# The output projection of a hybrid decoder layer as seven block products, with one sum of weight blocks made on chip

## What is computed

```python
g_nsa, g_sgu = jnp.split(jax.nn.sigmoid(merge_gl), 2, axis=-1)
merged = g_nsa * (o_nsa @ w_branch_nsa[l]) + g_sgu * (o_sgu @ w_branch_sgu[l])
mix = merged @ w_out[l]                                     # 512 x 1024 by 1024 x 1024
h = layer_norm(DEEPNORM_ALPHA * h + mix, ln1_g[l], ln1_b[l])
ffn = (jax.nn.silu(h @ w_ffn_gate[l]) * (h @ w_ffn_up[l])) @ w_ffn_down[l]
h = layer_norm(DEEPNORM_ALPHA * h + ffn, ln2_g[l], ln2_b[l])
```

## Time and profile before

| | |
|---|---|
| median of 3 runs | 712.57 us (712.55 to 713.74) |
| the profiled execution | 713.21 us, span 711.5 us |
| TensorE busy | 700.4 us (98%) |
| VectorE busy | 567.5 us (80%) |
| ScalarE busy | 352.0 us (49%) |
| GpSimd busy | 151.2 us (21%) |
| moved by DMA | 73.84 MB, mean 104 GB/s |
| mean granted TensorE clock | 0.996 |

### The profile page before, as it was taken

The page is one execution under the profiler, slowest core; times in us unless marked ns, Lnnn a source line. Parts: engine busy times, 40 slices in busy tenths (PEclk is TensorE's granted clock), DMA queues, the critical chain, the costliest instruction groups (busy, mean ns, idle before and its releaser), DMA issues.

```text
span 711.5 us, 11496 instructions
## 1 busy us (share of the span) xinstructions
PE 700.4 (98%) x4232; PEld 622.9 (88%) x4232; DVE 567.5 (80%) x918; ACT 352.0 (49%) x552; POOL 151.2 (21%) x167
## 2 busy tenths in 40 slices
PE   8999999999999999999999999999999999999995
PEld 7888988878888988888899899999999998888884
DVE  6885499787788785675889598999898886977877
ACT  6462777457777778222534244444544344145600
POOL 2942970422132210000000222222222210000001
PEclk9999999999999999999999999999999999999998
DMA  9612343111101205536532133233223328400102
GB/s 314 229 45 67 112 119 119 60 59 60 41 20 60 59 1 161 195 119 236 148 90 67 52 119 110 67 118 118 80 96 118 118 78 306 185 23 0 60 31 88
DMA packets 55716, 73.84 MB, mean 104 GB/s; under 512 B 4096, under 2 KB 40704, under 8 KB 55552
## 3 DMA queue, kind: packets, MB, share of 16 engines
q1 hardware_dynamic: 55392, 72.19, 30.6%
q0 software_dynamic: 144, 1.05, 0.7%
q10 hardware_dynamic: 144, 0.13, 0.1%
HBM read 70.21 MB, written 2.10 MB: 102 GB/s over the span
## 4 chain that ended last, share of the span: by engine, by line
PE 96%; DVE 2%; DMA 0%; ACT 0%; issue 0%; DVEq 0%; SPq 0%; ACTq 0%
PE ps L1981 65%; PE ps L2430 10%; PE ps L2064 5%; PE ps L2448 5%; PE ps L1993 4%; PE ps L1989 3%; PE ps L1990 3%; PE ps L2003 1%; PE ps L2421 0%; DMA stage<-in_w_in 0%; DVE ptl L1252 0%; PE ps L2164 0%; PE ps L2165 0%; DVE wl L1252 0%; DVE prob L1533 0%
## 5 line engine op out<-in xcount | busy, mean ns | idle before, releaser
L1981 PE MATMUL ps<-xh,wh 128*128 128x256 f32 (+1 forms) x416 | 135.0, 325 | 0.0
L1981 PE MATMUL ps<-xh,wl 128*128 128x256 f32 (+1 forms) x416 | 131.7, 317 | 0.0
L1981 PE MATMUL ps<-xl,wh 128*128 128x256 f32 (+1 forms) x416 | 131.6, 316 | 0.0
L1981 PE MATMUL ps<-ath,wh 128*128 128x256 f32 (+1 forms) x280 | 86.1, 307 | 0.0
L1981 PE MATMUL ps<-ath,wl 128*128 128x256 f32 (+1 forms) x280 | 86.0, 307 | 0.0
L1981 PE MATMUL ps<-atl,wh 128*128 128x256 f32 (+1 forms) x280 | 86.0, 307 | 0.0
L1981 PEld LDWEIGHTS ps<-xh,wl 128*128 128x128 f32 x416 | 79.3, 191 | 5.4
L1981 PEld LDWEIGHTS ps<-xh,wh 128*128 128x128 f32 x416 | 79.5, 191 | 3.1
L1981 PEld LDWEIGHTS ps<-xl,wh 128*128 128x128 f32 x416 | 79.5, 191 | 3.1
L1252 DVE TENSOR_TENSOR wl<-stage,wh 128x512 fp32r<-128x512 f32 (+2 forms) x73 | 64.6, 897 | 4.9 <-ACT wh L796 2.8
L1242 DVE TENSOR_TENSOR wl<-stage,wh 128x2048 fp32r<-128x2048 f32 (+1 forms) x19 | 43.1, 2267 | 27.8 <-ACT wh L793 19.6
(11 more groups left out here) (374 smaller groups left out, 1741.4 us busy)
## 6 DMA issues: line engine op xcount, KB each, us to landing
stage<-in_w_ffn_gate SPq DMA_DIRECT2D x22, 512.0 KB, 4.5
stage<-in_w_ffn_up SPq DMA_DIRECT2D x22, 512.0 KB, 4.5
stage<-in_w_in SPq DMA_DIRECT2D x20, 512.0 KB, 4.1
stage<-in_w_ffn_down SPq DMA_DIRECT2D x14, 512.0 KB, 4.2
quad_raw<-in_w_in SPq DMA_DIRECT2D x8, 512.0 KB, 9.4
stage<-in_w_out SPq DMA_DIRECT2D x8, 512.0 KB, 4.6
quad_raw<-in_w_ffn_down SPq DMA_DIRECT2D x4, 1024.0 KB, 10.1
arena<-in_x_t SPq DMA_DIRECT2D x8, 256.0 KB, 5.5
```

What stands on the lines that cost most here:

```text
L1981: return pe.matmul(out, (sh, sh, sl)[i], (mh, ml, mh)[i], start=start and i == 0, stop=stop and i == 2)
```

## The change

With merged tokens in two halves and its channels in two halves (blocks S), and `w_out` in four blocks B11, B12, B21, B22 (first index: channels), the product is made from seven block products of 24 matmuls instead of eight. In the order of TensorE, product 1 is S11 B11, product 2 is S12 B21, product 3 is s1 (B11 + B12), product 4 s2 times the sum B22 + B12 + B11, product 5 s4 B22, product 6 s3 (B22 + B12), product 7 S22 times B21 + that sum. `s1` to `s4` are sums or differences of merged blocks, made by VectorE. Results are added into `y` by twelve steps on VectorE (`take`), one of them from a copy of product 1 that ScalarE makes (`first_product`), because product 4 adds onto it in the same banks.

The sums of weight blocks are made by accumulating DMAs of GpSimd (`more`, `more_rows`; each waits for the one before), from `w_out` or from a block on chip. B22 + B12 is copied to `t_3` by SP, the sum of three is made in place on chip. Where a low part is made by DMA, as `second_l` is already, ScalarE writes the negated rounded block first (`negated`): so for products 4 and 7 and for `first_l`. That is eight accumulating DMAs instead of one.

Tiles 2 and 3 are both transposed in the last of the first four FFN tiles, tile 3 in its middle. The `up` tiles of the first FFN unit wait for the last sums out of banks 2 and 3 (`in_out` 14). The loops over `c` of ScalarE and VectorE are written out. SP's and ScalarE's queues are re-ordered as shown.

```diff
@@ SP
             load(U_BRANCH + 2, 0, nsa_rows(512))
-            load(U_BRANCH + 3, 1, rows4(sgu_d, 1, 0, 512, 512))
+            sp.wait_ge(st_done, 4)
+            out_rows(t_sums, 1, 1, 0)
             sp.wait_ge(o_end, PAIRS)
             sp.dma_start(y[:, :, :], x_d).then_inc(x2_arrived, 16)
-            with sp.Fori(0, 2) as c:
-                for kh in range(2):
-                    load(2 * c + U_OUT + kh, kh, rows4(wout_d, kh, kh, 512 * c, 512))
+            load(U_BRANCH + 3, 1, rows4(sgu_d, 1, 0, 512, 512))
+            sp.wait_ge(w_lo, U_BRANCH + 3)
+            out_rows(stage[0][:, :], 0, 0, 2)
+            sp.wait_ge(more_in, 16)
+            for i in range(2):
+                part = slice(1024 * i, 1024 * i + 1024)
+                sp.dma_start(t_3[:, part], t_sums[:, part]).then_inc(raw_arrived[1], 16)
+            sp.wait_ge(mg_ok, 4)
+            out_rows(b_21, 1, 0, 3)
+            load(U_FFN + 1, 1, rows8(up_d, 1, 0))
+            sp.wait_ge(part_lo, 12)
+            load(U_FFN, 0, rows8(gate_d, 0, 0))
+
+            sp.wait_ge(s_sum, 8)
             sp.wait_ge(mg_lo, KD)
...
@@ GpSimd
+            def more(n, dst, src):
+                if n > 1:
+                    pool.wait_ge(more_in, 16 * (n - 1))
+                pool.dma_start(dst, src, accum_op=ALU.add).then_inc(more_in, 16)
...
+            pool.wait_ge(part_lo, 9)
+            more_rows(1, t_sums, 0, 1)
+            pool.wait_ge(raw_arrived[1], 64)
+            more_rows(2, t_sums, 0, 0)
+            pool.wait_ge(part_lo, 10)
+            pool.dma_start(stage[0][:, :].rearrange("p (k n) -> p k n", k=4), wout_d[:, 0:4, 512:1024],
+                           accum_op=ALU.add).then_inc(second_in, 16)
+            pool.wait_ge(part_lo, 11)
+            more(3, b_21, t_sums)
             pool.wait_ge(second_neg, 1)
+            more(4, M_SLOT[0][1], t_sums)
+            pool.wait_ge(second_neg, 2)
+            more(5, M_SLOT[0][1], b_21)
+
+            pool.wait_ge(second_neg, 3)
+            pool.dma_start(first_l[:, :], stage[0][:, :], accum_op=ALU.add).then_inc(second_in, 16)
...
@@ ScalarE
+            late_split(U_BRANCH + 2, 0)
+            out_t_hi(2, t_sums, arrived_in=(0, 64))
+            for f in range(4):
+                merged_hi(f)
+            late_split(U_BRANCH + 3, 1)
+            act.wait_ge(w_used, U_BRANCH + 3)
+            out_t_hi(0, stage[0][:, :], arrived_in=(2, 64))
+            out_t_hi(3, b_21, arrived_in=(3, 64))
+            for f in range(4, 7):
+                merged_hi(f)
+            act.wait_ge(second_in, 16)
+            act.wait_ge(w_used, U_BRANCH + 4)
+            act.copy(M_SLOT[1][0], stage[0][:, :]).then_inc(part_hi, 1)
+            merged_hi(7)
+            act.wait_ge(more_in, 32)
+            act.wait_ge(in_used, 8)
+            negated(M_SLOT[0][1], t_sums)
+            out_s_hi("s1", 6)
+            out_t_hi(0, t_sums, 2)
+            out_s_hi("s2", 7)
+            act.wait_ge(in_used, 9)
+            act.copy(first_product, ps[:, 0:2, :]).then_inc(bank_out, 1)
+            out_s_hi("s4", 8)
+            act.wait_ge(in_used, 10)
+            out_s_hi("s3", 5)
+            out_t_hi(1, t_3, arrived_in=(1, 64))
+            act.wait_ge(more_in, 48)
+            act.wait_ge(in_used, 11)
+            negated(M_SLOT[0][1], b_21)
+            out_t_hi(0, b_21, 3)
+            act.wait_ge(w_arrived[0], arrived(U_FFN)[1])
+            act.wait_ge(part_lo, 13)
+            negated(first_l[:, :], stage[0][:, :])
...
             root(0)
+            split_to(first_h[:, :], U_FFN, 0, U_FFN)
             act.wait_ge(w_arrived[1], arrived(U_FFN + 1)[1])
-            act.mul(second_l[:, :], stage[1][:, :], -1.0).then_inc(second_neg, 1)
-            hi(second_h[:, :], stage[1][:, :]).then_inc(w_hi, 1)
+            negated(second_l[:, :], stage[1][:, :])
             root(1)
             ht_hi_of(0)
+            act.wait_ge(more_in, 80)
+            hi(second_h[:, :], stage[1][:, :]).then_inc(w_hi, 1)
             ht_hi_of(1)
             root(2)
-            split_to(wh[:, 0, :], U_FFN + 2, 0, U_OUT + 3)
+            act.wait_ge(in_used, 14)
+            split_to(wh[:, 0, :], U_FFN + 2, 0, U_FFN)
             ht_hi_of(2)
             root(3)
             ht_hi_of(3)
@@ VectorE
...
+            out_t_lo(1, stage[0][:, :], 12)
+            out_s_lo("s1", 13)
+            out_s(7, "s2", M_S["s1"], merged(0, 0))
...
+            dve.wait_ge(in_used, 11)
+            take(8, 0, 1, a_banks, ALU.subtract, True)
+            for m in range(2):
+                moments(m, 0)
+            dve.wait_ge(ln_arrived, 32)
+            for m in range(2):
...
+                take(9 + m, m, 1, ps[:, 4 + m:5 + m, :], ALU.add)
...
                 norm(m)
-                if m == 1:
-                    ht_lo_of(0)
+            dve.wait_ge(in_used, 13)
+            take(11, 2, 1, a_banks, ALU.subtract)
+            take(12, 2, 0, a_banks, ALU.add, True)
+            ht_lo_of(0)
+            ht_lo_of(1)
+            dve.wait_ge(in_out, 11)
+            for m in (2, 3):
+                moments(m, 1)
+            for m in (2, 3):
...
+                take(11 + m, m, 0, ps[:, m:m + 1, :], ALU.add)
...
+                norm(m)
             ht_lo_of(2)
             ht_lo_of(3)
@@ TensorE
+            pe.wait_ge(mg_lo, 4)
+            pe.wait_ge(br_prod, 12)
+            pe.wait_ge(part_lo, 10)
+            out_product(0, (0, 0), 0, True).then_inc(in_used, 1)
+            pe.wait_ge(part_lo, 11)
+            out_product(3, (0, 1), 2, True, by_k=True).then_inc(in_used, 1)
+            pe.wait_ge(br_prod, 16)
+            pe.wait_ge(part_lo, 12)
+            pe.wait_ge(xt_lo, 13)
+            out_product(1, M_S_AT["s1"], 4, True).then_inc(in_used, 1)
+            pe.wait_ge(part_hi, 13)
+            pe.wait_ge(more_in, 64)
+            pe.wait_ge(xt_lo, 14)
+            pe.wait_ge(bank_out, 5)
+            out_product(0, M_S_AT["s2"], 0, False).then_inc(in_used, 1)
+            pe.wait_ge(xt_lo, 15)
+            pe.wait_ge(in_out, 6)
+            out_product(2, M_S_AT["s4"], 4, False, (0,)).then_inc(rows_done, 1)
+            out_product(2, M_S_AT["s4"], 4, False, (1,)).then_inc(in_used, 1)
+            pe.wait_ge(part_lo, 13)
+            pe.wait_ge(xt_lo, 16)
+            pe.wait_ge(in_out, 8)
+            out_product(1, M_S_AT["s3"], 0, False).then_inc(in_used, 1)
             h_transposed(0)
-            last_rows(2, 1)
-            last_rows(3, 0)
+            pe.wait_ge(part_hi, 15)
+            pe.wait_ge(more_in, 80)
+            out_product(0, (1, 1), 2, True, (0,)).then_inc(rows_done, 1)
+            pe.wait_ge(in_out, 10)
             h_transposed(1)
-            last_rows(3, 1)
+            out_product(0, (1, 1), 2, True, (1,)).then_inc(in_used, 1)
...
                     if half == 0:
                         pe.wait_ge(w_lo, U_FFN + b + 1)
-                        pe.wait_ge(mg_lo, KD + MT + 2 * b + 2)
+                        pe.wait_ge(in_out, 12 + 2 * b)
...
                     for f in range(2):
-                        if half == 0 and (b, f) in h_transposed_at:
-                            h_transposed(h_transposed_at[b, f])
+                        if (half, b, f) == (0, 1, 1):
+                            h_transposed(2)
+                            ffn_tile(b, f, gh, gl, tok, range(4))
+                            h_transposed(3)
+                            ffn_tile(b, f, gh, gl, tok, range(4, KD))
+                            continue
```

More of the change, by code:

```diff
@@ new lines, in out_t_lo, with out_s_lo @@
+            def out_t_lo(slot, raw_t, hi_count):
+                dve.wait_ge(part_hi, hi_count)
+                h, l = M_SLOT[slot]
+                lo(l, raw_t, h).then_inc(part_lo, 1)
+            def out_s_lo(name, count):
+                dve.wait_ge(xt_hi, count)
+                at = M_S_AT[name]
+                lo(x_block(xl, *at), M_S[name], x_block(xh, *at)).then_inc(xt_lo, 1)
+            dve.wait_ge(sig_ok, 2)
+            for f in range(4):
+                gated(0, f, 0)
+            split(U_BRANCH + 2, 0)
@@ new lines, in _ @@
+            out_t_lo(2, t_sums, 9)
+            for f in range(4):
+                merged_sum(0, f)
+                merged_lo(f)
+            dve.wait_ge(mg_ok, 4)
+            out_s(5, "s3", merged(0, 0), merged(1, 0))
+            split(U_BRANCH + 3, 1)
+            dve.wait_ge(sig_ok, 4)
+            for f in range(3):
+                gated(1, f, 0)
+            out_t_lo(0, stage[0][:, :], 10)
+            gated(1, 3, 0)
+            out_t_lo(3, b_21, 11)
+            for f in range(3):
+                merged_sum(1, f)
+                merged_lo(4 + f)
@@ L1596, in moments @@
+            merged_sum(1, 3)
+            dve.wait_ge(mg_ok, KD)
+            out_s(6, "s1", merged(1, 0), merged(1, 1))
+            merged_lo(7)
+            out_t_lo(1, stage[0][:, :], 12)
+            out_s_lo("s1", 13)
+            out_s(7, "s2", M_S["s1"], merged(0, 0))
+            dve.wait_ge(s_sum, 7)
```

(38 more changed lines are left out.)

198 lines of the change are left out of this document (106 added, 92 removed).

## The result

The changed kernel takes 721.78 us (median of 4 runs, 720.51 to 722.65) beside 713.09 us for the kernel before on the same chip (712.55 to 713.74): ratio 1.0117 [1.0105, 1.013]. It is slower by 8.7 us. The forecast was 719.0 with a range of 711.5 to 726.5, so direction and range held, and the loss was forecast 2.8 us too small. In the profiled executions (722.65 and 713.21 us) the second token half of the first FFN unit begins at 383.92 us instead of 374.55: +9.37 of the +9.44 are there, ahead of the mark.

The account below looks back on a forecast made before the run. TensorE's unbroken work was taken to bound the kernel. 5.44 us saved, against waits of 0.4, 2.2 and 5.5, gave +2.6; accumulations' 3.8 made +6.4 on 712.57: 719.0 us, range 711.5 to 726.5.

Parts of the forecast that it names:

- What would show it: Trace signs: 168 block matmuls, TensorE pauses ahead of product 4, at second transposition and first FFN matmul, late row-3 root.
- TensorE saves 5.4: Block products on TensorE: eight blocks of 24 matmuls become seven, at 0.227 us each, 5.4 us less.
- Branch stage, +0.2 and +0.2: Before the FFN: TensorE waits 0.2 us ahead of product 1 and 0.2 for product 2's last merged tile.
- Accumulations, +3.8 ahead of product 4: GpSimd's chained accumulating DMAs, slowed by loads beside them, make TensorE wait 3.8 us (0 to 9.8) ahead of product 4.
- 4.5 for the loads: Accumulation chain: 3 MiB of loads between 299 and 311 occupy the DMA engines 9 us, half falling on the accumulations.
- The rule behind the 4.5: DMA engines shared evenly: half of each load's time, about 3 us per MiB, falls on the accumulation beside it.
- Clock: TensorE's clock: half rate considered only after a stop over 5 us, adding 5.4 in product 4; not in the sum.
- the second rival: Ahead of product 4: accumulations far slower, 724 to 726 us, possibly 5.4 more at half clock; chance 0.20.
- Row tiles: From product 5 to the FFN's second token half: TensorE waits on VectorE and ScalarE, 2.2 plus 5.5 us.
- The third rival: Row tiles: table load and roots come when VectorE asks, waits shrink 1.3 and 3.0, accumulations hidden, 710.9 us; chance 0.15.
- The rival on the faster side: Same as the third rival: ScalarE's queue does not hold the row tiles, -1.7 us, 710.9; chance 0.15.

Follow-up runs that it names:

- run 11: Changed kernel with `up` block later, roots ahead of the block copy, early table load, earlier takes, GpSimd accumulations back to back, `x` early: 711.77 us, ratio 0.9983.
- run 4: Changed kernel with the first `up` block's load moved behind those of the LayerNorm vectors: 716.69 us, ratio 1.0047.
- run 1: Changed kernel with ScalarE's square root of row tile 3 ahead of its copy of transposed tile 2: 718.62 us, ratio 1.0068.
- run 2: Changed kernel with product 4's low part made by VectorE instead of ScalarE's negation and an accumulating transfer: 717.41 us, ratio 1.0058.
- after: The changed kernel itself, without further edits, against the kernel before: 721.78 us, ratio 1.0117.
- run 3: Changed kernel with an unused square root on ScalarE ahead of product 4's wait, to load the table early (adds tile `warm`): 721.60 us, ratio 1.0107.
- run 9: Changed kernel with `up` block and `x` later, roots ahead of the block copy, early table load, earlier takes, GpSimd accumulations back to back: 713.15 us, ratio 1.000.
- run 10: Changed kernel with `up` block and `x` later, roots ahead of the block copy, earlier takes, GpSimd accumulations back to back, no early table load: 713.18 us, ratio 1.000.
- run 5: Changed kernel with the first `up` block loaded later and row tile 3's root ahead of the copy of tile 2: 713.26 us, ratio 1.000.
- run 6: Changed kernel with the `up` block later, row tile 3's root first, and the table load in idle time: 714.09 us, ratio 1.002.
- run 8: Changed kernel with the `up` block later, row tile 3's root first, and `x` loaded behind the second SGU block: 713.89 us, ratio 1.0012.
- run 7: Changed kernel with `up` block later, row tile 3's root first, early table load, and product 7's last two sums taken before row tile 2: 714.21 us, ratio 1.0016.

## Why the prediction was right, and where it was off

The mechanism held: every pause that "What would show it" lists is in the trace, and none of the things that would have made it wrong. The 2.8 us that it was short are nearly all one term that it had at nothing, the clock. By its terms:

- **TensorE saves 5.4.** 24 matmuls fewer, as said; run 11 shows what is left of it once most waits are gone: F is 3.3 earlier than before and F to mark is 1.8 longer (14.88 for 13.07), together -1.4, so some 2 us still go ahead of F and 1.8 behind it.
- **Branch stage, +0.2 and +0.2.** A merged tile takes 2.70 us (290.46 to 293.16, from one product with the gate to the next) for 2.73. Product 1 begins at 316.44, 0.48 later than before, for 0.2. TensorE's step ahead of product 2's last tile is 1.49 us from start to start (323.69 to 325.18), less one matmul of 0.23 a wait of 1.3, not 0.2, and for a reason that I had not given: I had VectorE's splits ahead of it, the chain shows ScalarE's copy of the block in the stage buffer, whose accumulation took 11.7 us.
- **Accumulations, +3.8 ahead of product 4.** The landings came as forecast. With its 4.5 for the loads the second was due at 316.2, the block in the stage buffer at 322.1, the third at 326.8; they landed at 316.5, 322.0 and 326.8. The fourth, 8.1 + 1.4 = 9.5, took 9.6. Product 4 was due at 332.8 + 3.8 = 336.6 (336.3, had the 0.3 of room been taken off) and began at 337.13. What the forecast didn't ask is who else waits for the late block in the stage buffer: ScalarE's queue did, and product 2 with it, 1.3 for 0.2. That moved waiting from product 4 (2.9, from 333.97 to 337.13) to product 2 and added little, as product 4 waits for a time set by the transfers. The rule behind the 4.5, half of each load on the accumulation beside it, fitted in sum and not load by load, which is luck: it gives the `up` block 1.5 us, and without it the second accumulation was 3.4 shorter and the third landed 2.5 earlier (run 4). An accumulation that reads HBM took 8.5 us the first time, near the 8.1 that the forecast let each take. Why 1 MiB in that place costs so much is only as far explained as that the DMA engines are busy all the time there and the transfers in flight take longer.
- **Clock.** This is the step that failed: I put the loss of clock into the second rival, for a stop of over 5 us, and had 0 for it in the forecast. Stops of 2.8 and 2.9 us brought it. It cost 1.7 us in product 4, and from product 4 to F it is 27.3 us for a forecast 25.7; it cost 0.9 in the fourth transposition (1.95 for 1.06), all of it left at the mark. With 0.5 for the start of product 4 that makes 1.6 + 0.9 + 0.5 = 3.0 us, by which the mark was later than forecast. Runs 1 and 2 show that a loss goes when its stop goes, and run 4 that a stop of 2.9 us can stand without one. Of seven stops of 2.5 us or more at these two places in the traces of after and of runs 1 to 4, six have the clock below full behind them, and in run 2 that cost nothing.
- **Row tiles.** From start to start, less one matmul: second transposition 1.1 for 1.0; first FFN matmul 0.9 for 1.2; `up` tiles 1.2 for 1.3; fourth transposition 3.0 for 3.0. At the second half itself it is 0.5 for 1.2, as TensorE's half tile was slowed into that wait. F to mark is 19.5, forecast 18.6, the difference being the clock; it is 18.6 in runs 2 and 4. The table load does what I said (VectorE waits 2.06 us for row 0's root behind it), but hiding it gave no time that can be measured (runs 9 and 10, with the slower matmuls that came with the edit). The third rival took 1.3 off for it, out of a wait that it had put at 1.0.
- **The rival on the faster side** had the right cause (ScalarE's root), and was right to want the accumulations hidden as well: with the root in time alone the kernel was still 5 us slower (run 1), with the accumulations hidden alone 3.4 (run 4). Both together gave no change (run 5), and with the table load as well 714.09 (run 6), not its 710.9. The 711.77 of run 11 is close to that number, but needed GpSimd's order and more edits, which the rival didn't have.

What stays open: why `x` late delays the accumulations more than it helps the branch stage (run 8) I read from the traces alone, why the tile `warm` goes with slower matmuls on `oth`, which may be part of what runs 6 and 7 lose against run 5, and when a stop of nearly 3 us brings the lower clock.

## What to carry to other kernels

A sum made by a transfer is not free work: with all DMA engines busy it took 12.1 us here beside loads and 8.7 with one load fewer. So count the queue's megabytes by stage, and move any load that isn't wanted soon out of that stage before judging the change. Read in-order queues of engines off the critical path for short instructions that stand behind long ones; one square root behind one copy cost 3 us here. Price a stop of TensorE of nearly 3 us at its length or at up to 1.7 us more, and look whether the slow matmuls behind it are waited for. And see whether an edit that is meant to move one instruction moves a tile as well.

## What the runs showed of the hardware

- An accumulating transfer of 1 MiB took 8.0 us before, 8.5 when the first of the chain ran (290.86 to 299.4), and 9.6 to 12.1 with other transfers beside it. Reading HBM made it longer by 1 us at most: 8.5, and 8.7 (304.40 to 313.1) with the `up` load gone, for 8.0 and 7.7 (issued at 346.75, after) from a block on chip.
- While accumulations and loads share the DMA engines, their share is 1.0 and more, at 205 to 231 GB/s from 309 to 325 us, where loads alone reached 369.
- The granted clock was 0.82 to 0.84 around and behind a stop of 2.8 us, 0.72 behind one of 2.9, and 1.00 behind those of 1.1 and behind one of 1.8 (run 9). In run 4 it was 1.00 behind one of 2.9 as well. A stop that was removed took its slow matmuls with it in each of runs 1, 2 and 4.
- Matmuls of 512 columns that read `oth` stood 0.233 us apart in the six kernels with the tile `warm`, 0.227 in the seven without.
